# Fetching the experts' token rows by indirect transfers, with the gate applied at the output eviction and two experts scattered at once

## What is computed

```python
def moe(x, router_w, wg, wu, wd):
    logits = (xt @ router_w).astype(jnp.float32)
    top_v, top_i = lax.top_k(logits, TOP_K)
    gates = jax.nn.softmax(top_v, axis=-1)
    combine = jnp.sum(jax.nn.one_hot(top_i, N_EXPERTS) * gates[..., None], axis=1)
    for e in range(N_EXPERTS):
        out = out + combine[:, e:e + 1] * swiglu(xt, wg[e], wu[e], wd[e])
```

## Time and profile before

| | |
|---|---|
| median of 3 runs | 1193.41 us (1193.22 to 1206.66) |
| profiled execution | 1204.01 us, its span 1202.2 us |
| mean granted TensorE clock | 0.954 of 2.4 GHz |
| TensorE, DVE, ACT busy | 93%, 66%, 54% of the span |
| start of the first expert, end of the last scatter | 718.7 us, 1184.1 us |

### The profile page before, as it was taken

One profiled execution on the slowest core, in us unless ns is written; L12 is line 12 of the kernel. 1 busy time (PEld: TensorE's weight loads), 2 busy tenths in 40 slices (PEclk: granted clock), 3 DMA queues, 4 the chain that ended last, 5 costly groups with the idle time before them and its releaser, 6 DMA issues.

```text
span 1202.2 us, 19971 instructions
## 1 busy us (share of the span) xinstructions
PE 1121.9 (93%) x7698; PEld 1040.3 (87%) x7698; DVE 795.1 (66%) x1125; ACT 645.1 (54%) x864; POOL 19.9 (2%) x38
## 2 busy tenths in 40 slices
PE   6998997899999998998987889999999999999995
PEld 5998985799999998998866869898989899889994
DVE  5689633565645555976533457885888788768884
ACT  5676433454334445674432327765766667566762
POOL 0010000000000000000000000000000000000000
PEclk9999999899999999999997859998999999889998
DMA  8454598545555554544685417994989598759871
GB/s 330 144 166 124 158 357 317 211 156 189 182 178 179 187 178 132 176 135 158 239 323 209 169 48 271 341 349 139 366 297 353 206 354 305 289 196 363 304 268 38
DMA packets 64276, 273.00 MB, mean 227 GB/s; under 512 B 7328, under 2 KB 7584, under 8 KB 63552
## 3 DMA queue, kind: packets, MB, share of 16 engines
q1 hardware_dynamic: 62352, 264.33, 62.1%
q0 software_dynamic: 1408, 7.12, 1.7%
q10 hardware_dynamic: 432, 0.38, 0.1%
HBM read 265.83 MB, written 5.98 MB: 226 GB/s over the span
## 4 chain that ended last, share of the span: by engine, by line
PE 71%; DVE 15%; ACT 6%; DMA 4%; issue 3%; SPq 0%; DVEq 0%; ACTq 0%
PE bank L596 10%; PE bank L597 10%; PE bank L598 10%; PE bank L593 10%; PE bank L594 9%; PE bank L595 9%; DVE wl L1402 4%; DMA ring<-dense 3%; PE bank L880 3%; ACT wh L1025 2%; PE bank L621 2%; DVE rstd L1397 2%; PE bank L881 1%; DVE wl L1670 1%; DVE sq L1413 1%
## 5 line engine op out<-in xcount | busy, mean ns | idle before, releaser
L1670 DVE TENSOR_TENSOR wl<-ring,wh 128x1408 fp32r<-128x1408 f32 x192 | 310.4, 1625 | 62.6 <-ACT wh L1268 62.4
L1402 DVE TENSOR_TENSOR wl<-ring,wh 128x1024 fp32r<-128x1024 f32 x170 | 207.2, 1223 | 193.1 <-ACT wh L1025 192.2
L1268 ACT ACTIVATE wh<-ring 128x1408 fp32r<-128x1408 f32 x189 | 261.0, 1381 | 87.8 <-PE bank L598 87.5
L593 PE MATMUL bank<-xh,wh 128*128 128x264 f32 x928 | 273.6, 295 | 27.9 <-DVE xl L1418 14.1
L594 PE MATMUL bank<-xl,wh 128*128 128x264 f32 x928 | 269.0, 290 | 0.0
L595 PE MATMUL bank<-xh,wl 128*128 128x264 f32 x928 | 268.1, 289 | 0.0
L1025 ACT ACTIVATE wh<-ring 128x1024 fp32r<-128x1024 f32 x170 | 178.9, 1056 | 165.3 <-PE bank L595 142.7
L597 PE MATMUL bank<-wh,xl 128*128 128x352 f32 (+4 forms) x736 | 245.0, 333 | 0.0
L593 PEld LDWEIGHTS bank<-xh,wh 128*128 128x128 f32 x928 | 180.2, 194 | 36.7 <-issue 23.1
L594 PEld LDWEIGHTS bank<-xl,wh 128*128 128x128 f32 x928 | 180.7, 195 | 0.0
L595 PEld LDWEIGHTS bank<-xh,wl 128*128 128x128 f32 x928 | 180.1, 194 | 0.0
(11 more groups left out here) (222 smaller groups left out, 1394.1 us busy)
## 6 DMA issues: line engine op xcount, KB each, us to landing
ring<-experts SPq DMA_DIRECT2D x192, 704.0 KB, 5.9
ring<-dense SPq DMA_DIRECT2D x234, 512.0 KB, 3.8
o_k<-kv POOLq DMA_DIRECT2D x2, 1024.0 KB, 4.4
o_v<-kv POOLq DMA_DIRECT2D x2, 1024.0 KB, 7.8
x<-xT SPq DMA_DIRECT2D x2, 528.0 KB, 5.0
o_y<-sq SPq DMA_DIRECT2D x4, 264.0 KB, 2.1
gatew<-gate_w POOLq DMA_DIRECT2D x2, 512.0 KB, 8.2
mem<-memT SPq DMA_DIRECT2D x1, 1024.0 KB, 13.3
```

The lines of the kernel that those rows point to most:

```text
L593: mm(out, s_hi, m_hi, start=start, stop=False)
L1268: A(wh[:, jj % NBUF, :], eraw(jj % ESLOTS), ACT.Copy).then_inc(ehi_ready, 1)
L1402: V.tensor_tensor(wl[:, k % NBUF, 0:UNIT], raw(u), wh[:, k % NBUF, 0:UNIT].bitcast(F32), ALU.subtract)\
L1670: V.tensor_tensor(wl[:, jj % NBUF, :], eraw(jj % ESLOTS), wh[:, jj % NBUF, :].bitcast(F32), ALU.subtract)\
```

## The change

- **Tokens.** The rows are no longer normed before routing: `xg` is `x` times the gain, made by ACT during the `mo` projection. The factor 1/rms of each token is found later (`sst`, 24 matmuls with one column) and carried along as a value of the slot. Half of the logits and of the turned tokens come before the last pair of the projection, half behind it. POOL writes the turned rows to DRAM (`token_rows`).
- **Gather.** For each expert a one-hot matrix of slots (`sel`) times token number, gate weight and 1/rms (`val`) gives each slot's three numbers (`slot_numbers`: I0 and I1 the number, I2 the others). POOL fetches the 128 rows of a slot block from DRAM by an indirect transfer (`pick`), a pair ahead; TensorE turns them, 16 transposes for a pair.
- **1/rms** is applied as the scale of silu and in the multiplication `hidden`; **the gate** at the copy of D0 and D1 (ACT high part, DVE low part, new: `out_low`).
- **Scatter.** One scatter for a pair, in the first expert of the next: 32 fp32r matmuls, high and low parts of two outputs times 0/1 matrices.
- **Turns** are four instead of three (T0 and T1 behind group 2, T2 behind group 3, T3 behind scatter or gather).
- The blocks beyond the first 128 slots are one pass each instead of one for all; with these inputs none runs.

The core of the diff:

```diff
@@ tensor @@
             def gather(p, num):
-                pe.wait_ge(gsel_ready, p + 1)
+                pe.wait_ge(picked_loaded, 32 * p + 32)
...
-                            mm(out, tokh[0:rows, t, f0:f0 + P], slots, start=(t == 0), stop=False)
-                            i = mm(out, tokl[0:rows, t, f0:f0 + P], slots, start=False, stop=(t == 2))
+                            i = nc.tensor.transpose(b[:, (2 * c + side) * CAP:(2 * c + side + 1) * CAP], picked[:, side, f0:f0 + P], ident)
...
-                    full(mm(b[:, 0:T], eo[:, c * P:(c + 1) * P], scat, start=True, stop=True), n)
+                    for side in range(2):
+                        for part in range(2):
+                            i = mm(b[:, 0:T], eout[:, side, part, c * P:(c + 1) * P], scat[:, side, :], start=(side + part == 0),
+                                   stop=(side + part == 2))
+                    full(i, n)
...
+            for s in range(3):
+                project_pair("mo", l, s, xhi, xlo, T)
+            logits(0, 4)
+            turn_tokens(0, 0, 4)
+            project_pair("mo", l, 3, xhi, xlo, T)
+            logits(4, 6)
+            logits(6, KC)
+            turn_tokens(1, 4, KC)
...
                 turn_hidden(num, 0)
-                if not first:
-                    turn_scatter(v - 1, num)
+                turn_hidden(num, 1)
                 group(3)
-                turn_hidden(num, 1)
-                if not first:
-                    scatter(num, before)
+                turn_hidden(num, 2)
+                if side == 0 and not first:
+                    scatter(p - 1, num, before)
                 if side == 1 and not last:
                     gather(p + 1, num)
-                turn_hidden(num, 2)
+                turn_hidden(num, 3)
...
+                slot_numbers(ps, "I0", 0, 2, 0, 1)
+                slot_numbers(ps, "I1", 2, NE, 0, 1)
+                if ps is main:
+                    pe.wait_ge(val_ready, 1)
+                slot_numbers(ps, "I2", 0, NE, 1, 3)
@@ scalar @@
+                if side == 0:
+                    act.wait_ge(now_ready, p + 1)
                 upto(4)
...
                 upto(15)
                 turned(num, 0)
-                if not first:
-                    scattered(num)
+                turned(num, 1)
                 upto(16)
                 silu(3)
+                turned(num, 2)
                 upto(19)
-                turned(num, 1)
                 if side == 1 and not last:
                     gathered(num)
-                turned(num, 2)
+                turned(num, 3)
                 upto(23)
                 for u in range(2):
...
-                    read(A(eo[:, u * 512:(u + 1) * 512], bank(n)[:, :], ACT.Copy), n)
+                    A(eout[:, side, 0, u * 512:(u + 1) * 512], bank(n)[:, :], ACT.Copy, scale=now[:, side, 1:2]).then_inc(eout_ready, 1)
                     upto(27)
@@ vector @@
                 upto(15)
                 turned_low(v, num, 0)
+                turned_low(v, num, 1)
                 upto(18)
                 hidden(3)
-                turned_low(v, num, 1)
+                turned_low(v, num, 2)
                 upto(19)
-                if not first:
-                    combine(num)
+                if side == 0:
+                    if not first:
+                        combine(num)
+                    scatter_matrix(p)
                 if side == 1 and not last:
                     gathered_low(p + 1, num)
-                turned_low(v, num, 2)
-                scatter_matrix(v)
+                turned_low(v, num, 3)
+                upto(25)
+                out_low(0)
+                upto(26)
+                out_low(1)
                 upto(27)
...
+                if not first:
+                    wait_read(dve, *prior("D1"))
+                pair_scalars(p, p0)
                 expert(p, 0, a, prior, first, last)
@@ gpsimd @@
+            def pick(k, v):
+                for side in range(2):
+                    pool.indirect_dma_start(picked[:, side, :], None, rows, bass.IndirectOffsetOnAxis(idx[:, v + side:v + side + 1], 0))\
+                        .then_inc(picked_loaded, 16)
```

More of the change, by code:

```diff
@@ L162, in bank_plan @@
         out += [("pv", l, m) for m in range(4, KC)]
[L163 to L164 removed]
         if l % 2 == 0:
+            out += [("mo", l, m) for m in range(KC)]
+            out += [("ssq", 3 * l + 2)]
             out += [("kf", l, u) for u in range(2)]
@@ L259, in trunk_kernel @@
         coef = sb("coef", [P, 6, DEPTH * RC])
+        with nc.sbuf_tensor("expert_out", [P, 4 * D], F32R) as eout_t:
+            pass
         kv = sb("kv", [P, KC * NM + MC * D])
@@ L517, in trunk_kernel @@
         main = Pass(NT0, 0, NE)
-        extra = Pass(main.end, NE, NE * (MAXB - 1))
+        passes = [main]
+        for b in range(1, MAXB):
+            passes.append(Pass(passes[-1].end, NE * b, NE))
         @block.sync
@@ L850, in _, with logits @@
[L850 to L856, removed]
+            def logits(c0, c1):
+                nn = [tiles[("lg", l, t)] for t in range(3)]
+                bb = [take_bank(n) if c0 == 0 else bank(n) for n in nn]
+                for c in range(c0, c1):
+                    pe.wait_ge(xg_ready, c + 1)
+                    for t, (t0, rows_t) in enumerate(TOK):
+                        i = mm(bb[t][0:rows_t, 0:NE], xg[:, c, t0:t0 + rows_t], rw[:, c, :], start=(c == 0), stop=(c == KC - 1))
+                        if c == KC - 1:
+                            full(i, nn[t])
@@ new lines, in _ @@
+            for s in range(3):
[6 more added lines that the diff above has]
+            turn_tokens(1, 4, KC)
+            n = tiles[("sst", l)]
+            b = take_bank(n)
+            pe.wait_ge(sq_ready, KC * (3 * l + 3))
+            for t, (t0, rows_t) in enumerate(TOK):
+                for c in range(KC):
+                    i = mm(b[0:rows_t, t:t + 1], sq[:, c, t0:t0 + rows_t], ones[:, 0:1], start=(c == 0), stop=(c == KC - 1))
@@ L979, in run_pass @@
                 pair(p1, ps.last, ps.earlier(p1), last=True)
-                turn_scatter(2 * p1 + 1, ps.after)
-                scatter(ps.after, block_of(ps.last, "b"))
+                scatter(p1, ps.after, block_of(ps.last, "b"))
             for t in range(3):
@@ L1301, in silu @@
                         wait_read(act, *num(f"U{g - 2}"))
-                    read(A(esg[:, g % 2, :], bank(n)[:, 0:GW], ACT.Silu), n)
+                    read(A(esg[:, g % 2, :], bank(n)[:, 0:GW], ACT.Silu, scale=now[:, side, 2:3]), n)
+                if side == 0:
+                    act.wait_ge(now_ready, p + 1)
                 upto(4)
@@ L1829, in _ @@
             for b in range(MAXB):
-                step(V.tensor_tensor(wts[:, :, b, :], oh, second, ALU.add))
+                step(V.tensor_tensor(val[:, :, NE * b:NE * (b + 1), 1], oh, second, ALU.add))
+            signal(val_ready)
+            for j in range(NBUF):
+                elow(0, j)
+            slot_scalars(main)
+            dve.wait_ge(kv_written, 32 * DEPTH)
             run_pass(main)
```

333 lines of the change are left out of this document (206 added, 127 removed).

## The result

The changed kernel takes 1217.7 us, the median of 4 runs (1213.94 to 1218.49), against 1197.1 us for the kernel before (4 runs on the same chip, 1193.22 to 1206.66). The ratio is 1.0187 with a 95% interval of 1.0139 to 1.0235: slower, by an amount on the edge of the 2%. The prediction was 1209.0 with a range of 1186 to 1228; its main case, 1199 to 1217, was missed by 0.7 us. The profiled execution took 1213.94 us with a span of 1212.1, that of before 1204.01 with 1202.2, so the trace has 9.9 us to account for.

The account below looks back on a forecast made before the run. TensorE was taken as the bound (busy 93% of the span, 71% of the chain), with DVE close behind in the experts. 1202.2 - 1.2 routing - 10.3 expert stage + 16.4 clock = 1207.1, plus 1.8 around the span: 1208.9 us; range 1186 to 1228.

Parts of the forecast that it names:

- main case: Whole kernel: the forecast proper, 1199 to 1217 us, chance 0.45.
- The expert stage: All eight experts with the last scatter: 455.1 us against 465.4 before, -10.3, then +16.4 for lower clock.
- From an expert's start to T2: Eight expert starts up to the last turns behind group 3: 252.2 us, plus 8.8 for late units.
- T2 to down projection: In each expert: 6.5 us in two, 6.7 in three, 8.9 in three that scatter, 59.8 in all.
- The order on ACT: T2's copy ahead of units 16 to 18 delays hidden(3), T3 and the down projection, taking back most of 50 us freed.
- The clock: Idle TensorE gaps before the down projections lower the clock: 2.05 us per expert, +16.4 in all, bounds 0 and 27.
- The order on DVE: Where experts meet, out_low(1) ahead of unit 26 loses 0.65 us; at a pair's start 1.4 more, three times.
- The scatter and the X turns: In the expert stage: 32 scatter matmuls per pair take 3.8 us, 16 transposes some 1.8.
- the routing stage: Before the experts: first expert starts at 712 to 721 us, 717.5 taken, -1.2 against before.
- The gaps cost no clock: Rival: TensorE's idle gaps in the experts leave the clock up, 1192.5 us; chance 0.20.
- The work saved arrives: Rival: high parts aren't held up, down projections start 2.3, 2.7 and 5.1 us after T2, 1161 us; chance 0.13.
- The slow rival: Over 2% slower: each gap before the down projection loses 3.4 us of clock, 1223 and up to 1228; chance 0.22.

Follow-up runs that it names:

- experiment 1: Changed kernel with T2's copy on ACT put back behind the high parts of units 16 to 18: 1169.34 us, ratio 0.9809 to the kernel before.
- experiment 6: Kernel before with only T1's copy on ACT moved ahead of unit 16's high part: 1256.59 us, ratio 1.0512 to the kernel before.
- experiment 2: Changed kernel with dummy matmuls filling TensorE's gap ahead of T3, or ahead of C5's matmuls where it scatters: 1204.05 us, ratio 1.0098 to the kernel before.
- experiment 3: Changed kernel with out_low(1) behind unit 26's low part on DVE and ACT's early wait for pair scalars removed: 1206.41 us, ratio 1.0126 to the kernel before.
- experiment 4: Changed kernel with only the first pair's slot numbers before the first expert, the rest inside it: 1209.29 us, ratio 1.0125 to the kernel before.
- experiment 5: Changed kernel with the edits of experiment 1, experiment 3 and experiment 4 together: 1156.93 us, ratio 0.9675 to the kernel before; repeated at 1155.02 us.
- experiment 7: Kernel of experiment 5 plus dummy matmuls ahead of I0 (4) and I2 (13) in the routing stage: 1153.79 us, ratio 0.9659 to the kernel before.

## Why the prediction held, and where it didn't

**The range held the time; the central value was 8.7 us low.** The profiled execution gained 9.9 us where 4.9 was forecast. By parts:

- **The expert stage came out as worked out.** 455.1 + 16.4 = 471.5 was forecast, 470.3 measured. From an expert's start to T2, late units included: 252.2 + 8.8 = 261.0 forecast, 263.4 measured. T2 to down projection: 59.8 forecast, 59.4 measured. Last scatter: 5.5 forecast, 5.9 measured (1188.21 to 1194.09). Down projections, start to start: 128.8 + 16.4 = 145.2 forecast, 141.6 measured (17.2 to 18.5 each). The terms are off by up to 3.6 us either way, so that the sum is within 1.2 is in part luck.
- **The order on ACT** is shown to be the cause by experiments 1 and 6, one undoing it where it was made and the other making it where it wasn't. It took back nearly all that the gather and the scatter had freed: between T2 and the down projections 47.7 us are free in experiment 1 (73.9 before, 26.2 there; some 50 was forecast), and the order cost the stage 45.4.
- **The clock.** All eight gaps lost it, as forecast (at 2.05 us each, the mean of the near rows). The eight down projections took 141.6 us against 129.6 in experiment 1: 12.0 us, 1.5 each. With T3 and the scatter it is 14.9, 1.9 each (experiment 2: 12.7 from seven gaps). The term (16.4) was right in kind and 1.5 us too large; it was put into the down projections alone, where 12.0 of it fell. The Trainium skill (TensorE: Matmul & The Clock Gate, Why this matters for your kernels) warns of idle gaps between bursts of matmuls; the five gaps of 3.88 and 5.62 us agree. In the three scattering experts the idle time comes in two pieces (2.65 and 1.11 us) with eight matmuls between them, each shorter than the gap that the page names, and the clock fell there too.
- **The order on DVE** (0.65 and 1.4 each forecast, 0.70 and about 1.1 measured) is shown by experiment 3.
- **The scatter and the X turns**: 32 matmuls in 4.1 to 4.4 us against 3.8, 16 transposes in 1.91 against 1.8.
- **The step that failed is the routing stage**: "First expert at 712 to 721; I take 717.5, because the engine is mostly idle there: -1.2". It was 723.75, +5.1. The engine was not idle but busy for 11.7 of 13 us at 1.2 GHz. I priced `I2`'s 48 records at 5 to 8 us; they took 11.7, 0.24 each. And I1's 36 records (8.76 us) stand ahead of I2 in TensorE's queue; I had DVE's list as the bound there (11 us) and put I1 nowhere: from the position matmuls to I2 it was 16.8 us. The position matmuls themselves ended at 689.9, 2 to 6 us earlier than forecast, which by luck hid part of this. Experiment 4 shows it: without most of those records the first expert starts at 710.44. These 6.3 us are more than the whole error of the profiled sum (5.0).
- **The timed runs did not stand where the sum stood.** The rest of the 8.7 us is between the profiled execution (1213.94) and the median (1217.7) of the change. The forecast held that without a long gather nothing was left that could run at either clock. But the three executions that weren't profiled have a mean granted clock of 0.943 to 0.944 against 0.952, and spans of 1215.8 to 1216.7 against 1212.1. So the share of the time at 1.2 GHz still varied; in which stretches is not shown.

**The rivals.** "The gaps cost no clock" is refuted: all eight did. "The work saved arrives" is refuted for this kernel by the waits of 5.62 us, and is what experiment 1 turned on: 1161 was its price, 1169.34 the measurement. The slow rival wanted 3.0 us and more per gap; it was 1.9 (14.9 in eight). Where the result did come near 2% slower, the routing stage took it there.

## What to carry to other kernels

When an engine works in order, moving one short copy ahead of long work makes that work wait for the copy's input; follow the queue on to the next engine before counting any gain, here 45 us for one line. Work taken off the bound engine is worth only as much as the engines behind it are early, so list for every engine what stands between the freed moment and the next thing the bound engine needs. Many tiny matmuls are not free: count their records, their queue position and the clock they will run at.

## What the runs showed of the hardware

- **The clock fell here while the profile had TensorE busy.** In the changed kernel it went from 1.00 to 0.50 at 686.4 us, with TensorE busy for 2.00 of 2.00 us in the windows on both sides, behind 48 one-column records (4.11 us). In experiment 5 it fell at 731.8, right behind 36 three-column records; in experiment 4 at 731.2, in their midst; both times the engine had been busy for over 10 us. In experiment 7 it fell at 704.3, behind 12 two-column records and 2.4 us after a gap of 0.41 us. What in these stretches brings the fall is not shown; no run took them apart.
- **Once low, it can stay low under full load.** The old gather, busy for 14.92 of 14.92 us, ran at 0.50 throughout in experiment 6, three times of three; in experiment 7 eight 256-column records from 690.35 on (3.76 us) had it back at 0.98 in the window from 694 to 696 us. That the two of three gathers at a lower clock explain the spread of the kernel before (1187 to 1207 us over all its runs) fits its trace, and wasn't shown.
- **The price of a narrow fp32 record** is 0.086 us at full clock for the one-column sums (48 in 4.11), and for the one- and two-column slot numbers 0.24 at 1.2 GHz (12 in 2.94, 48 in 11.75) but 0.15 at full clock for two columns (12 in 1.76, experiment 7).
